# All u keys of PEER in 512-column matmuls, their cross half copied by ScalarE, unsplit low parts, and smaller moves in the norms

## What is computed

```python
def peer_ffn(xn, w_q, sub_keys, u, v):
    B, S, D = xn.shape
    T = B * S
    t = xn.reshape(T, D)
    q = (t @ w_q).reshape(T, PEER_HEADS, 2, PEER_HALF)
    s = jnp.einsum('thpd,hpnd->thpn', q, sub_keys).astype(jnp.float32)
    s_top, i_top = lax.top_k(s, PEER_TOPK)
    cand_s = (s_top[:, :, 0, :, None] + s_top[:, :, 1, None, :]).reshape(T, PEER_HEADS, PEER_TOPK * PEER_TOPK)
    cand_i = (i_top[:, :, 0, :, None] * PEER_KEYS + i_top[:, :, 1, None, :]).reshape(T, PEER_HEADS, PEER_TOPK * PEER_TOPK)
    best_s, pos = lax.top_k(cand_s, PEER_TOPK)
    ids = jnp.take_along_axis(cand_i, pos, axis=-1).reshape(T, PEER_HEADS * PEER_TOPK)
    gates = jax.nn.softmax(best_s, axis=-1).reshape(T, PEER_HEADS * PEER_TOPK)
    n_chunks = T // PEER_TOKEN_CHUNK

    def chunk(args):
        x_c, ids_c, g_c = args
        act = jax.nn.gelu(jnp.einsum('td,ted->te', x_c, u[ids_c]), approximate=False)
        return jnp.einsum('te,ted->td', g_c.astype(x_c.dtype) * act, v[ids_c])

    y = lax.map(chunk, (t.reshape(n_chunks, PEER_TOKEN_CHUNK, D),
                        ids.reshape(n_chunks, PEER_TOKEN_CHUNK, -1),
                        gates.reshape(n_chunks, PEER_TOKEN_CHUNK, -1)))
    return y.reshape(B, S, D)
...
    h = rmsnorm(x, ln_mix_g)
    proj = h @ w_in
...
    y_lru = rg_lru(lru_x, lru_wa, lru_ba, lru_wx, lru_bx, lru_lambda) * jax.nn.gelu(lru_gate, approximate=False)
...
    y_attn = moba_attention(q.reshape(shp), k.reshape(shp), v.reshape(shp)).reshape(B, S, D_ATTN)
    mixed = jnp.concatenate([rmsnorm(y_lru, gn_lru_g), rmsnorm(y_attn, gn_attn_g)], axis=-1)
    x = x + mixed @ w_out
    x = x + memory_cross_attention(rmsnorm(x, ln_cross_g), rmsnorm(mem, ln_mem_g), w_cq, w_ck, w_cv, w_co)
    x = x + peer_ffn(rmsnorm(x, ln_ffn_g), peer_wq, peer_subkeys, peer_u, peer_v)
...
    return rmsnorm(x, ln_final_g)
```

## Time and profile before

| | us |
|---|---|
| time, median of 3 runs | 965.06 (963.64 to 965.83) |
| the profiled execution's time | 963.7 |
| its span | 961.9 |
| u keys on PE | 274.5 to 643.9 |
| GpSimd's scatters | 249.0 to 629.5 |

### The profile page before, as it was taken

The page is one execution under the profiler, slowest core; times in us unless marked ns, Lnnn a source line. Parts: engine busy times, 40 slices in busy tenths (PEclk is TensorE's granted clock), DMA queues, the critical chain, the costliest instruction groups (busy, mean ns, idle before and its releaser), DMA issues.

```text
span 961.9 us, 18013 instructions
## 1 busy us (share of the span) xinstructions
PE 952.4 (99%) x6807; PEld 914.7 (95%) x6807; DVE 807.4 (84%) x1571; ACT 543.3 (56%) x953; POOL 481.4 (50%) x315
## 2 busy tenths in 40 slices
PE   8999999999999999999999999999999999999997
PEld 8898899999999999999998888889999999999997
DVE  6989875547999999999988787777899998989896
ACT  7776555555556555554555565555555555555555
POOL 1001001010588888888788888827478872223110
PEclk9999999999999999999999999999999999999999
DMA  9789865344557777878778878879999999999992
GB/s 317 221 312 338 299 231 200 108 132 132 176 100 193 194 207 178 211 164 205 205 185 211 196 170 196 201 203 342 326 360 345 369 356 365 357 357 359 381 321 74
DMA packets 134265, 235.61 MB, mean 245 GB/s; under 512 B 38624, under 2 KB 87520, under 8 KB 133824
## 3 DMA queue, kind: packets, MB, share of 16 engines
q1 hardware_dynamic: 97552, 208.66, 64.3%
q0 software_dynamic: 36224, 25.70, 14.3%
q10 hardware_dynamic: 432, 0.57, 0.2%
HBM read 216.38 MB, written 17.97 MB: 244 GB/s over the span
## 4 chain that ended last, share of the span: by engine, by line
PE 95%; DVE 3%; ACT 2%; DMA 0%; issue 0%; ACTq 0%; DVEq 0%
PE acc L1439 15%; PE acc L1703 11%; PE bank L1703 11%; PE bank L1668 9%; PE bank L1637 8%; PE bank L1636 8%; PE bank L1638 8%; PE bank L1704 5%; PE acc L1704 5%; PE bank L1669 5%; PE acc L1421 3%; PE acc L1422 2%; PE bank L1621 1%; PE bank L1545 1%; DVE wsp L894 1%; PE bank L1567 1%
## 5 line engine op out<-in xcount | busy, mean ns | idle before, releaser
L478 POOL DMA_INDIRECT wmap<-gate,widx x192 | 320.0, 1667 | 91.3 <-issue 60.5
L762 ACT ACTIVATE hl<-raw 128x1024 fp32r<-128x1024 f32 x192 | 203.1, 1059 | 98.6 <-PE bank L1669 41.6
L1144 DVE TENSOR_TENSOR hl<-raw,hl 128x1024 fp32r<-128x1024 f32 x99 | 121.1, 1224 | 28.6 <-ACT hl L762 28.1
L1636 PE MATMUL bank<-xt,hl 128*128 128x256 f32 x480 | 135.9, 283 | 0.0
L1637 PE MATMUL bank<-xt,hl 128*128 128x256 f32 x480 | 135.8, 283 | 0.0
L1638 PE MATMUL bank<-xt,hl 128*128 128x256 f32 x480 | 135.7, 283 | 0.0
L1151 DVE TENSOR_TENSOR hl<-raw,hl 128x512 fp32r<-128x512 f32 x186 | 119.4, 687 | 17.0 <-ACT hl L762 15.8
L501 POOL DMA_INDIRECT vg<-v,idx_v x48 | 73.6, 1534 | 116.7 <-DVE acc_s L1285 96.8
L1703 PE MATMUL acc<-whl,hl 128*128 128x416 f32 x380 | 121.4, 370 | 0.0
L1703 PE MATMUL bank<-whl,hl 128*128 128x416 f32 x380 | 120.9, 368 | 0.0
L1668 PE MATMUL bank<-xt,hl 128*128 128x512 f32 x288 | 102.4, 399 | 0.0
(11 more groups left out here) (306 smaller groups left out, 2377.4 us busy)
## 6 DMA issues: line engine op xcount, KB each, us to landing
raw<-u_t SPq DMA_DIRECT2D x128, 512.0 KB, 4.7
raw<-v SPq DMA_DIRECT2D x128, 512.0 KB, 5.7
wmap<-zeros SPq DMA_DIRECT2D x6, 2048.0 KB, 11.8
wblk<-wmap SPq DMA_DIRECT2D x62, 192.0 KB, 5.7
wraw<-w_in SPq DMA_DIRECT2D x9, 1024.0 KB, 9.3
wraw<-w_pq SPq DMA_DIRECT2D x8, 1024.0 KB, 5.3
wraw<-w_ck SPq DMA_DIRECT2D x4, 1024.0 KB, 8.1
wraw<-w_cv SPq DMA_DIRECT2D x4, 1024.0 KB, 8.3
```

What stands on the lines that cost most here:

```text
L478: nc.gpsimd.indirect_dma_start(out=wmap, out_offset=bass.IndirectOffsetOnAxis(ap=set_ranks(widx, k)[:, h, r:r + 1], axis=0), in_=set_ranks ...
L762: nc.scalar.activation(eslot(k, 0, second), raw[:, k // 2, k % 2], ACT.Copy).then_inc(ready, 1)
L1144: V.tensor_tensor(eslot(k, 1, second), raw[:, k // 2, k % 2], eslot(k, 0, second).bitcast(F32), ALU.subtract).then_inc(ready, 1)
L1636: pe.matmul(dst, uh[:, c], xt[:, c, 0], start=(c == 0), stop=False)
```

## The change

All 128 u keys take the wide form, in one loop. For keys 0 to 119 (`AIDED = 120`) ACT copies the cross half of the bank to SBUF (`copy_cross`, tile `xprod`), and DVE's `wide_sum` adds the other half of the bank and that copy (an add of 256 columns); keys 120 to 127 keep the reduction. The gelu reads `acc` for every key and stands one key behind in ACT's order up to key 106. `split_low_halves` is gone: every u key's low part is one instruction of 1024 columns. Routing parts come every two keys, the last batch of gates is parted in two, and what hung on the end of the routing moves from key 88 to 108 (`STAGE_KEY`), 92 to 107 (`WEAVE`), 95 to 109 (`ROUTE0`). GpSimd also waits for the sum of key 119 ahead of the block loads, since `xprod_late` lies where `wblk` does.

Ahead of the u keys: the first norm's square root takes mean and epsilon in its own scale and bias, without DVE's step; tile 1 of the first norm and of the norm ahead of PEER is scaled in two halves, and PE's transposes start on the first; the recurrence's gate matmuls wait for the low parts in pairs; `cross_low(2)` stands ahead of the split of `U_CQ + 3` on DVE.

```diff
-BATCHES = ((0, 0, 1), (0, 1, 3), (0, 3, 5), (0, 5, PH), (1, 0, 3), (1, 3, PH))
+BATCHES = ((0, 0, 1), (0, 1, 3), (0, 3, 5), (0, 5, PH), (1, 0, 3), (1, 3, 5), (1, 5, PH))
 EARLY = 2
 PARTS0 = 14
-HALVES = 0
-WEAVE = 92
-WIDE0 = 80
+WEAVE = 107
+AIDED = KEYS - 8
+LATE_TMP = 108
 RUN = 7
 GAINS = 6
-ROUTE0 = 95
+ROUTE0 = 109
+STAGE_KEY = 108
+LAG_END = 106
...
-            return -(-3 * (n - PARTS0 + 1) // 2) - 1
+            return 2 * (n - PARTS0 + 1) - 1
...
-                if j == 88:
+                if j == STAGE_KEY:
...
+            pool.wait_ge(s_us, AIDED)
...
+            def first_deviation(t):
+                act.wait_ge(s_sq, t + 1)
+                nc.scalar.activation(stat[:, RS + t:RS + t + 1], stat[:, SS + t:SS + t + 1], ACT.Sqrt, bias=tcol[:, 3:4],
+                                     scale=1.0 / D).then_inc(s_std, 1)
...
+            def copy_cross(j):
+                act.wait_ge(s_um, j + 1)
+                if j >= 2:
+                    act.wait_ge(s_us, j - 1)
+                nc.scalar.activation(cross_copy(j), ubank(j)[:, T:2 * T], ACT.Copy).then_inc(s_uc, 1)
...
             def gelu(j):
-                if j < WIDE0:
-                    act.wait_ge(s_um, j + 1)
-                    u = ubank(j)
-                else:
-                    act.wait_ge(s_us, j - WIDE0 + 1)
-                    u = acc[:, j % 2]
+                act.wait_ge(s_us, j + 1)
...
+                if j < AIDED:
+                    copy_cross(j)
...
-                if j >= WIDE0:
+                if 0 < j <= LAG_END:
+                    gelu(j - 1)
+                if j >= LAG_END:
                     gelu(j)
...
                     link(V.reciprocal(rd, rd))
-                    V.tensor_scalar(dst[:, t], src[:, t], rd, None, ALU.mult).then_inc(s_xs, 1)
+                    if (n, t) in HALVED:
+                        q = slice(0, D // 2)
+                        V.tensor_scalar(dst[:, t, q], src[:, t, q], rd, None, ALU.mult).then_inc(s_xsh, 1)
+                        q = slice(D // 2, D)
+                        V.tensor_scalar(dst[:, t, q], src[:, t, q], rd, None, ALU.mult).then_inc(s_xs, 1)
+                    else:
+                        V.tensor_scalar(dst[:, t], src[:, t], rd, None, ALU.mult).then_inc(s_xs, 1)
...
+            cross_low(2)
             unit(U_CQ + 3)
-            cross_low(2)
...
-            def split_low_halves(k, ready, have):
-                dve.wait_ge(*have)
-                for n in range(2):
-                    q = slice(512 * n, 512 * n + 512)
-                    last = V.tensor_tensor(eslot(k, 1, False)[:, q], raw[:, k // 2, k % 2, q], eslot(k, 0, False)[:, q].bitcast(F32),
-                                           ALU.subtract)
-                last.then_inc(ready, 1)
...
             def wide_sum(j):
-                dve.wait_ge(s_um, j + 1)
-                if j >= WIDE0 + 2:
+                if j >= 2:
                     dve.wait_ge(s_ua, j - 1)
-                V.tensor_reduce(acc[:, j % 2, 0:T], ubank(j)[:].rearrange("p (a t) -> p t a", a=2), X, ALU.add).then_inc(s_us, 1)
+                if j < AIDED:
+                    dve.wait_ge(s_uc, j + 1)
+                    V.tensor_tensor(acc[:, j % 2, 0:T], ubank(j)[:, 0:T], cross_copy(j), ALU.add).then_inc(s_us, 1)
+                else:
+                    dve.wait_ge(s_um, j + 1)
...
-                if j >= WIDE0:
-                    wide_sum(j)
+                wide_sum(j)
                 if j == KEYS - 2:
                     a_low(0)
-                if HALVES <= j < KEYS - 4:
-                    split_low_halves(j % 4, s_ul, (s_uh, j + 5))
-                elif j < KEYS - 4:
+                if j < KEYS - 4:
                     split_low(j % 4, s_ul, (s_uh, j + 5))
...
-            pe.wait_ge(s_tl, 2 * DC)
             for mch in range(LC):
+                pe.wait_ge(s_tl, DC + 2 * mch + 2)
...
-                    pe.matmul(dst, uh[:, c], xt[:, c, 0], start=(c == 0), stop=False)
-                    pe.matmul(dst, uh[:, c], xt[:, c, 1], start=False, stop=False)
-                    last = pe.matmul(dst, ul[:, c], xt[:, c, 0], start=False, stop=(c == DC - 1))
+                    pe.matmul(dst, uh[:, c], flat(xt[:, c]), start=(c == 0), stop=False, skip_group_check=True)
+                    last = pe.matmul(dst[:, 0:T], ul[:, c], xt[:, c, 0], start=False, stop=(c == DC - 1), skip_group_check=True)
...
-            with pe.Fori(1, WIDE0 // 4) as it:
+            with pe.Fori(1, WEAVE // 4) as it:
                 for k in range(4):
                     pe.wait_ge(s_ul, it * 4 + (k + 1))
-                    pe.wait_ge(s_ua, it * 4 + (k - 3))
-                    u_key(k, bank[k][:, 0:T])
+                    pe.wait_ge(s_us, it * 4 + (k - 3))
+                    u_key(k, bank[k][:])
```

More of the change, by code:

```diff
@@ L56 @@
 ACT_SCALED = ((2, 1), (3, 0))
+HALVED = ((0, 1), (3, 1))
 WIDE_UNITS = tuple(range(U_GATE, U_V)) + tuple(range(U_CK, U_OUT))
@@ L145, in build @@
         sel = at("sel", m + 4352, [NS])
+        xprod = [at("xprod", 112 * K, [2, T]), at("xprod_late", m + 2304, [2, T])]
         wblk = at("wblk", m + 1280, [2, WBK, WT])
@@ L296, in build, with cross_copy @@
         wm = wmap.rearrange("(i j t) o -> i j (t o)", i=KEYS, t=WT)
+        def cross_copy(j):
+            return xprod[j >= LATE_TMP][:, j % 2]
         def ubank(j):
@@ L569, in _ @@
             warm_sqrt()
+            act.wait_ge(s_const, 10)
             for t in range(TT):
@@ L572, in _ @@
                 squares(0, t, xr, xs)
-                tile_deviation(0, t)
+                first_deviation(t)
             act.wait_ge(s_w0, 16)
@@ L911, in tile_norm @@
             def tile_norm(n, t, src, dst):
[L913 to L917, removed]
+                if n:
+                    dve.wait_ge(s_sq, TT * n + t + 1 if n < 2 else 2 * TT + 5 * (n - 2) + 3 + t + 1)
+                    ss = stat[:, SS + 2 * n + t:SS + 2 * n + t + 1]
+                    if n >= 2:
+                        link(V.tensor_reduce(ss, stat[:, QS + 4 * t:QS + 4 * t + 4], X, ALU.add))
+                    V.tensor_scalar(ss, ss, 1.0 / D, EPS, ALU.mult, ALU.add).then_inc(s_var, 1)
                 dve.wait_ge(s_std, norm_count(n, t))
@@ L1181, in route_part @@
                     ks = slice(TOPK * h, TOPK * h + TOPK)
-                    link(V.tensor_reduce(krow[:, t, 0:2, ks], eq[:], X, ALU.add))
-                    V.tensor_scalar(krow[:, t, 2, ks], topv[:, 2], topv[:, 2, 0:1], None, ALU.subtract).then_inc(s_rt, 1)
+                    V.tensor_scalar(krow[:, t, 2, ks], topv[:, 2], topv[:, 2, 0:1], None, ALU.subtract)
+                    V.tensor_reduce(krow[:, t, 0:2, ks], eq[:], X, ALU.add).then_inc(s_rt, 1)
             def gates(b):
@@ L1188, in gates @@
                 n, ks = h1 - h0, slice(TOPK * h0, TOPK * h1)
+                dve.wait_ge(s_rt, PH * t + h1)
                 last_batch = b == len(BATCHES) - 1
@@ L1388, in transposes @@
                 for t in range(TT):
-                    pe.wait_ge(s_xs, TT * n + t + 1)
+                    if (n, t) in HALVED:
+                        pe.wait_ge(s_xsh, HALVED.index((n, t)) + 1)
+                    else:
+                        pe.wait_ge(s_xs, TT * n + t + 1)
                     for c in range(DC):
+                        if c == DC // 2 and (n, t) in HALVED:
+                            pe.wait_ge(s_xs, TT * n + t + 1)
                         o = T * (c % 2) + P * t
@@ L1662, in route @@
                 last.then_inc(s_gm, 1)
-            def u_key_wide(slot, dst):
-                uh = eslot(slot, 0, False).rearrange("p (c i) -> p c i", c=DC)
-                ul = eslot(slot, 1, False).rearrange("p (c i) -> p c i", c=DC)
-                for c in range(DC):
-                    pe.matmul(dst, uh[:, c], flat(xt[:, c]), start=(c == 0), stop=False, skip_group_check=True)
-                    last = pe.matmul(dst[:, 0:T], ul[:, c], xt[:, c, 0], start=False, stop=(c == DC - 1), skip_group_check=True)
-                last.then_inc(s_um, 1)
-            for j in range(WIDE0, KEYS):
-                pe.wait_ge(s_ul, j + 1)
-                if j < WIDE0 + 4:
-                    pe.wait_ge(s_ua, j - 3)
-                else:
-                    pe.wait_ge(s_us, j - WIDE0 - 3)
-                u_key_wide(j % 4, ubank(j)[:])
+            for j in range(WEAVE // 4 * 4, KEYS):
+                pe.wait_ge(s_ul, j + 1)
+                pe.wait_ge(s_us, j - 3)
+                u_key(j % 4, ubank(j)[:])
                 if j == WEAVE:
@@ L1695, in v_key @@
                     if first and c >= 4:
-                        pe.wait_ge(s_us, KEYS - WIDE0 - 7 + c)
+                        pe.wait_ge(s_us, KEYS - 7 + c)
                     if first and c == 1:
```

16 lines of the change are left out of this document (8 added, 8 removed).

## The result

| | before | after |
|---|---|---|
| time, median of 5 runs | 963.74 us (963.57 to 965.83) | 985.05 us (983.68 to 987.22) |
| ratio, 95% interval | | 1.0221 (1.0210 to 1.0232) |
| the profiled execution's span | 961.9 | 983.6 |
| first u key, first v key on PE | 274.66, 643.93 | 273.79, 663.04 |
| GpSimd's scatters, first start to last end | 249.0 to 629.5 | 248.1 to 655.8 |

The change makes the kernel 21.3 us slower; 12.0 were predicted. The time of 985.05 lies inside the range that was given, 965 to 990.

The account below looks back on a forecast made before the run. PE's work was taken as the bound, with the scatter chain 0.9 us behind it. Longer scatters start the v keys 11.0 later, 12.0 with the restart: 963.7 + 12.0 = 975.7, on the median's scale 977.0; range 965 to 990.

Parts of the forecast that it names:

- The chain that binds: Beside PE in the u keys: scatters, landing, block loads, `weigh`, sum and `a_low` set when the v keys begin, 11.0 later.
- What holds a scatter: In the u keys: a scatter starting during a DVE split waits, to 1.10 after a whole split's start, 0.56 for a half.
- The size of that term: Scatters under whole splits in the u keys: 14 us of added delay taken, a little under the scaled 16.8.
- the ends 0 and 34: Limits of the scatters' added delay: 0 if they fall between the splits, 34 if held one per key for some 24 keys.
- The random value: Mean delay per u-key scatter if starts were random against the splits: 0.109 us for halves, 0.214 for whole splits.
- falling into step: Rival in the u keys: scatters run between splits, no more lengthening, time 963, limit 960.5; chance 0.19, 0.11 of it below 963.1.
- The lock at the end: After the routing parts: each scatter starts 0.13 inside the next split, one per key for some 24 keys, 21 us of delay.
- From the last scatter to the v keys: Ahead of the v keys: 13.5 us, with 5.00 until the scatters land and block loads of 5.5 to 6.0.
- its rival: DVE becomes the bound of the keys: an add of 0.70 makes a key 2.97 on DVE, time about 975; chance 0.05.
- SP's wait: For the staged gates, moved to key 108: loads behind it cost the u keys at worst one key, 2.8, covered at the seam.
- the 0.9 of slack: At the seam: v keys could begin at 643.0 but begin at 643.93; longer scatters pay for all but 0.9 us.
- the restart: At the first v keys, after PE stands still some 15 us: a slow start costing 0 to 2.0 us, 1 taken.

Follow-up runs that it names:

- experiment 1: The changed kernel with every u key's low part inside the loop made in two instructions of 512 columns; 968.04 us, ratio 1.0048 to the kernel before.
- experiment 2: The kernel before with every u key's low part in one instruction of 1024 columns, nothing else of the change; 1007.94 us, ratio 1.0456.
- mix: The changed kernel with SP's wait at key 112, low parts in two pieces beside routing parts, four elsewhere and after key 100; 964.38 us, ratio 1.0008.
- experiment 6: The changed kernel with SP's wait for the staged gates at key 112 instead of 108; 987.24 us, ratio 1.0241 to the kernel before.
- front_quarters: Number 7 with low parts in four pieces every third key and from key 80 on, two elsewhere; 964.36 us, ratio 1.0000.
- number 7: The kernel before with only the changes ahead of the u keys; 963.03 us against 963.97 for the kernel before, ratio 1.0001.
- experiment 5: The changed kernel with 80 matmuls of 128 columns on the identity ahead of the first v key; 983.94 us, ratio 1.0198 to the kernel before.

## Why the prediction was right in kind, and short in size

**The chain that binds: right.** PE's busy time did not change, the last scatter set the first `v_key`, and the sign followed. Experiments 1 and 2 show the whole split as the cause, from either side.

**What holds a scatter: right, and sharper than told.** I sorted the scatters of the u keys by the DVE instruction in which each starts and summed their delays. After, 60 that start in a whole split have 38.7 of delay, 13 that start in the `eq` comparison of a routing part (L1195, two SBUF inputs) have 6.3, and all others together less than 0.1; 46 of these start in the new add of a PSUM and an SBUF tile. That the add is short is not what spares them: in `mix` 45 scatters that start in a piece of a split of the same 256 columns, with two SBUF inputs, have 6.3 of delay (0.14 each, 0.49 at most). One place shows the three kinds. DVE, then GpSimd:

```profile
401.17 1.21 DVE L1170 TENSOR_TENSOR hl<-raw,hl 128x1024 fp32r<-128x1024 f32 x1
402.30 0.42 DVE L1313 TENSOR_TENSOR acc<-bank,xprod 128x256 f32<-128x256 f32 x1
...
404.04 0.69 DVE L1195 TENSOR_TENSOR eq<-posu,iota 128x512 f32<-128x512 uint32 x1
...
406.24 0.42 DVE L1313 TENSOR_TENSOR acc<-bank,xprod 128x256 f32<-128x256 f32 x1
```

```profile
402.12 1.69 POOL L486 DMA_INDIRECT wmap<-gate,widx  x1 [0.31 <-issue]
404.11 2.05 POOL L486 DMA_INDIRECT wmap<-gate,widx  x1 [0.30 <-issue]
406.46 1.55 POOL L486 DMA_INDIRECT wmap<-gate,widx  x1 [0.30 <-issue]
```

The first starts 0.95 into a split and is held 0.14, to 1.09 after the split's start; the second starts in the comparison and is held 0.50; the third starts in the add and is not held. By the Trainium skill (SBUF — State Buffer, "Who interferes with whom") a VectorE instruction with at most one SBUF input, outside its two-port modes, doesn't contend with GpSimd, and the trace agrees (46 scatters, 0.00 each). The inference in the same section of the Trainium skill, that an add or subtract of two tensors leaves the making of descriptors alone, finds no support here (60 scatters in whole splits, 0.65 each).

**The size of that term: the step that failed.** The prediction took 14 of added delay; it is 27.5, inside the ends 0 and 34. Three things went wrong in it. The random value, 0.214 for each of 180 scatters, is 38.5, and whole splits gave 38.7: I had scaled it by 0.89, the ratio of 0.097 to 0.109 of the kernel before, and that ratio did not carry over. I then took a value below the scaled one for a falling into step that did not come. And the `eq` instructions of the routing parts were left out; before, they cost 0.5 (L1180), after, 6.3 (L1195). Whole splits and `eq` together give 38.7 + 6.3 - 17.5 = 27.5. The lock at the end is within the 38.7: 9.2 of it lies after 608 us. So that the random value comes so near is partly luck, and it is no safe estimate: in experiment 1 the halves have 26.4 where it gives 20, and in experiment 2 the whole splits 65.8 where it gives 38.

**From the last scatter to the v keys: 13.5 predicted, 7.3 measured** (655.78 to 663.04). The scatters land after 2.19 instead of 5.00, and the blocks in 2.7 to 2.8 us instead of 5.5 to 6.0. The queues are nearly empty then (19 GB/s in the window 650 to 660; before, 218 GB/s while the last scatter lands). The path of before was measured among other transfers, and I carried it over into a gap without them. All twelve traces agree: the seven whose scatters end after the loads of the u keys wait 2.1 to 2.3 for the last landing, the five others 3.5 to 5.0. This took 6.2 back. That the time lies inside the range is partly luck, then: two errors of opposite sign met in it, and with the predicted 13.5 here it would have been 991.

**The rest held.** The first u key begins 0.87 earlier (1.1 predicted). A key takes 2.825 (16 of them 45.2), as forecast. DVE's add takes 0.42 and DVE kept up, so its rival fell. SP's wait cost the u keys 2.4 (369.0 against 366.6 in experiment 6; at most 2.8 predicted) and was covered, as experiment 6 shows. The sum: the scatters' start 0.9 earlier, 27.5 more of delay and 0.3 less in the pauses between scatters put the last scatter's end 26.3 later; less 6.2 on the path and the 0.9 of slack, the v keys begin 19.1 later; with the restart it is 21.7.

**What stays open.** Why halves in the changed kernel meet 30.8 us of delay in the u keys and in the kernel before 17.5, and why finer pieces added delay in `front_quarters` (24.3 against 16.7 in number 7): both may come from the phase between the scatters' 1.85 us and DVE's pattern, but no run changed the phase alone. Part of the second is in the trace: three scatters of `front_quarters`, at 285.19, 396.98 and 483.25, are held 1.02 to 1.43 across two or three pieces that follow one another, 3.6 of the 24.3. So the boundary between two pieces does not always let a waiting scatter go, as the prediction had it.

## What to carry to other kernels

Look for a chain that runs beside the busiest engine with almost no slack; it appears in no busy share, and here it turned a gain of 2 us into a loss of 21. A longer instruction on one engine can cost more than its own time where another engine waits for it to end: a whole split is 0.09 us shorter than two halves, and it cost 17. The waiting engine can lock to the other's period, as the scatters did. Bound such a term by the lock, and don't shave it; the random value was far too low in experiments 1 and 2. Durations of transfers taken from a busy stretch don't hold in an empty one.

## What the hardware showed that was not expected

An idle time of 2.5 us at the seam (experiment 1) cost as much in clock as one of 20.3: from the first `v_key` to the end 320.9 (968.0 - 647.1) and 320.6 against 318.0, so a wait of 2.5 us cost 5.4. But the length of the wait alone doesn't tell what it costs. The same 2.5 us in experiment 5, behind the added matmuls, left the granted clock at 1.00. In the u keys a wait of 1.7 (changed kernel) left it at 1.00, and one of 1.9 at the same place (experiment 5) was followed by 0.50 from 589 to 591.5. The 0.91 ahead of PEER's transposes left no slow stretch in the trace of before. No run here shows what decides.

The other surprise is the lock: GpSimd's scatters and DVE's splits kept the same step for 21 scatters without a miss.
